# Consuming gathered expert rows two by two instead of four by four

## The chip, the cores and the metric

The program runs on one core of one Trainium2 chip. The metric is the device time of one execution in microseconds; the median of three runs of the kernel before is 1976.25 us (1974.51 to 1980.7). Engines are called as in the profile: PE is TensorE, DVE is VectorE, ACT is ScalarE, POOL is GpSimd, SP is SyncE.

## What is computed

A decoder trunk of two layers over 256 positions of width 1024, all in float32. Layer 0 mixes tokens with a state-space mixer (S5) and a GLU, layer 1 with dilated window attention (3 groups of 16 heads). After each comes PEER, a mixer that picks 128 single-neuron experts per token out of 16384 and evaluates only those:

```python
def peer_ffn(h, w_q, sub_keys, u_tab, v_tab):
    ...
    idx = jnp.take_along_axis(cand_idx, pos, axis=-1)      # 8 heads x top 16 = 128 per token
    gate = jax.nn.softmax(best, axis=-1).astype(h.dtype)
    ...
    def chunk_fn(args):
        hc, ic, gc = args
        act = jnp.einsum('cd,ckd->ck', hc, u_tab[ic])
        return jnp.einsum('ck,ckd->cd', gc * jax.nn.gelu(act), v_tab[ic])
```

So each token needs the dot product of its h with 128 rows of u, a gelu, a gate, and the sum of 128 rows of v with those weights. Rows of u and v of one expert are stored beside each other, 2048 floats.

## The kernel before

The 256 tokens are two chunks of 128. PEER is done four times (layer 0 chunks 0 and 1, layer 1 chunks 0 and 1); these are phases 0 to 3. The experts' rows of one phase are gathered while the other engines do the next chunk's mixer: phase 0 beside the S5 mixer of chunk 1, phases 1 and 2 beside projections and attention of chunks 0 and 1, phase 3 beside little else.

**A gather** (POOL, L816) brings 128 expert rows, one per partition, 8 KB each, into one of 8 slots of `ring` (`RING`, 1 MB each). The partitions are 32 tokens by 4 experts: gather j of four (`QUAD`) serves tokens 32j to 32j+31, and the four gathers with the same n serve all 128 tokens with four experts each. A phase has 128 gathers, or rows, as this text calls them for short.

**A quad** is four gathers in a row. For each, DVE waits until it has landed and takes the dot products with `Hrep`, h copied to that layout (L839, 1024 elements). After the fourth, DVE multiplies the one-hot matrix `own` with the gates from `lay` into `S` (L849), ACT takes the gelu of the 128x4 dots (L644), DVE multiplies it into `S` (L852), and PE does 8 matmuls (L380): for each half of the 1024 columns and each j, a 128x32 stationary from `S` with 512 columns of the ring slot, accumulated in partitions 32j to 32j+31 of the PSUM tile `ps`. Semaphore `v_pe` counts quads done by PE. POOL waits for it before it gathers into the slots again, four slots at a time; DVE waits for it before it writes a buffer of `S` (there are two).

**The order** is written by hand and is the same on PE, ACT and DVE. Each engine's program has a `Gather` object, and `g.at(phase, n)` stands between the pieces of the mixer: it does all gather work up to tick n, two rows a tick, 64 ticks a phase. With quads, PE and ACT have something to do only at every second tick. Each engine runs its instructions in this order. In the projections (`project`, L412; QKV has 9 of 512 columns for each half of the heads) a tick stands before each; weights come in blocks of 2 MB through two buffers of `wt`, and SP issues a load when the projection before the last is done. In the attention heads a tick stands at every second head in chunk 0 and at every head in chunk 1; a head is scores (L535), mask and maximum on DVE (L1132), exp on ACT (L729), transposes on PE (L546), their copy on ACT (L737) and the product with V (L560). PE does in a row the transposes of one head, the V products of the one before and the scores of the next but one; then it waits for DVE and ACT. In the S5 stage DVE rotates (L950 to 956), scans (L965) and forms products (L982 to 985) for 8 tiles, four ticks to a tile.

**Top-k** of the next phase's experts runs on DVE in four quarters with four parts each (`top_k_part`); a tick stands before each part. After a quarter ACT copies the result to `lay` (16 copies, L690, and a cast, L693). ACT loads a table when it changes between functions (gelu, exp, sqrt). At the start of a phase PE and ACT spread h to `Hrep` (L397, L656).

Of the kernel before, what the change touches and what calls it, by code (L numbers as in the profile page):

```python
# [29 lines left out]
ALU = mybir.AluOpType  # L30
# [3 lines left out]
P = 128  # L34
D = 1024
SEQ = 256
NC = SEQ // P
# [50 lines left out]
def build(nc, x, gains, lam, b_in, c_out, d_skip, w_glu, w_qkv, w_o, w_q, keys, experts, consts,  # L88
          masks, out):
    ctx = ExitStack()  # L90
    with ctx:
        def sb(name, shape, dt=F32):
            return ctx.enter_context(nc.sbuf_tensor(name, shape, dt))

        def sem(name):
            return ctx.enter_context(nc.semaphore(name))
# [15 lines left out]
        dots = sb("dots", [P, 2, QUAD])  # L112
        gelus = sb("gelus", [P, 2, QUAD])
        S = sb("S", [P, 2, QUAD, TG])
        zs = sb("zs", [P, 5, PAIRS])
        stat = sb("stat", [P, 8])
        half_pi = sb("half_pi", [P, 1])
# [5 lines left out]
        ps = ctx.enter_context(nc.psum_tensor("ps", [P, 8, 512], F32))  # L123
# [5 lines left out]
        own = con[:, C_REP:C_REP + TG]  # L129

        def banks(a, b):
            return ps[:, a:b, :].rearrange("p b n -> p (b n)")

        def view(t, at, *shape):
            n = int(np.prod(shape))
            v = t[:, at:at + n]
            if len(shape) == 2:
                v = v.rearrange("p (a b) -> p a b", a=shape[0])
            if len(shape) == 3:
                v = v.rearrange("p (a b c) -> p a b c", a=shape[0], b=shape[1])  # L140
            return v

        def spread(ap, axis, shape):
            return ap.unsqueeze(axis).to_broadcast(shape)
# [48 lines left out]
        ring = view(ringmem, 0, RING, 2 * D)  # L193
# [41 lines left out]
        idx_ready = sem("idx_ready")  # L235
# [2 lines left out]
        landed = [sem(f"landed{i}") for i in range(RING)]  # L238
        dots_ready = sem("dots_ready")
        gelu_ready = sem("gelu_ready")  # L240
        s_ready = sem("s_ready")
        v_pe = sem("v_pe")
        peer_done = sem("peer_done")
# [124 lines left out]
        def _(pe):  # L368
            def slot(s):

                q, j = divmod(s, QUAD)
                if j < QUAD - 1:
                    return
                phase, n = divmod(q, QUADS)
                pe.wait_ge(s_ready, q + 1)
                if n == 0 and phase:
                    pe.wait_ge(peer_done, phase)
                for half in range(2):
                    for j in range(QUAD):
                        last = pe.matmul(ps[TG * j:TG * (j + 1), half, :], S[:, q % 2, j, :],  # L380
                                         ring[:, (QUAD * q + j) % RING,
                                              D + half * 512:D + (half + 1) * 512],
                                         start=(n == 0), stop=(n == QUADS - 1), skip_group_check=True)
                last.then_inc(v_pe, 1)

# [244 lines left out]
        def _(act):  # L630
# [6 lines left out]

            def slot(s):

                q, j = divmod(s, QUAD)  # L640
                if j < QUAD - 1:
                    return
                act.wait_ge(dots_ready, q + 1)
                act.activation(gelus[:, q % 2, :], dots[:, q % 2, :],  # L644
                               ACT.Gelu_apprx_tanh).then_inc(gelu_ready, 1)

            g = Gather(slot)

            def spread_h(phase):

                if phase:
                    act.wait_ge(dots_ready, QUADS * phase)
# [150 lines left out]
        @block.gpsimd  # L803
        def _(pool):
            pool.memset(WB.rearrange("p a b c -> p (a b c)"), 0.0).then_inc(zeroed, 1)
            pool.memset(CW.rearrange("p a b c -> p (a b c)"), 0.0).then_inc(zeroed, 1)
            pool.memset(half_pi[:, :], HALF_PI).then_inc(zeroed, 1)

            for s in range(2 * NC * STEPS):
                phase, at = divmod(s, STEPS)  # L810
                n, j = divmod(at, QUAD)
                if at % QSTEPS == 0:
                    pool.wait_ge(idx_ready, QUARTERS * phase + at // QSTEPS + 1)
                if s >= RING:
                    pool.wait_ge(v_pe, (s - RING) // QUAD + 1)
                pool.indirect_dma_start(  # L816
                    ring[:, s % RING, :], None, experts[phase // NC],
                    bass.IndirectOffsetOnAxis(ap=rows[:, phase % NC, j, n:n + 1], axis=0)
                ).then_inc(landed[s % RING], 16)
# [3 lines left out]
        def _(v):  # L823
            steps = [0]

            def link(ins):
                steps[0] += 1
                ins.then_inc(dve, 1)
                v.wait_ge(dve, steps[0])

            def slot(s):

                q, j = divmod(s, QUAD)
                phase, n = divmod(q, QUADS)
                c, b, i = phase % NC, q % 2, s % RING
                if n == 0:
                    v.wait_ge(hrep_ready, 2 * QUAD * phase + 2 * j + 2)
                v.wait_ge(landed[i], 16 * (s // RING + 1))
                last = v.tensor_tensor_reduce(ring[:, i, 0:D], ring[:, i, 0:D], Hrep[:, j, :],  # L839
                                              1.0, 0.0, ALU.mult, ALU.add, dots[:, b, j:j + 1])  # L840
                if j < QUAD - 1:
# [12 lines left out]

            g = Gather(slot)
# [1 line left out]
            def peer_end(phase):  # L857

                c = phase % NC
                g.at(phase, PAIRS_G)  # L860
                v.wait_ge(v_pe, QUADS * (phase + 1))
# [406 lines left out]
```

## Time and profile before

| | |
|---|---|
| median of 3 runs | 1976.25 us |
| profiled execution, its time | 1980.83 us |
| its span | 1979.0 us |
| PE busy (matmuls) | 1131.4 us, 57% |
| DVE busy | 1220.7 us, 62% |
| ACT busy | 319.6 us, 16% |
| POOL busy | 542.8 us, 27% |
| DMA moved | 685.21 MB, mean 346 GB/s |
| mean granted clock of PE | 0.729 |

Busy times are for the whole span and mix stages with different limits. A better reading is by stretches: what PE, DVE and DMA do in 50 us of one stage. Granted clock is the share of 2.4 GHz; its two levels are 0.50 (1.2 GHz) and 1.00 (2.4 GHz). A matmul of float32 operands appears as two records, so 8 matmuls are 16 records. In a timeline the brackets hold the idle time before the row and what ended it.

### The profile page before, as it was taken

The numbers are of one execution on the slowest core, as the hardware profiler recorded it, in microseconds if no ns is written. First come the engines' busy times: TensorE is split into PE (matmuls) and PEld (weight loads), VectorE is DVE, ScalarE is ACT, GpSimd is POOL, SyncE is SP. The second block draws the span as 40 slices with busy tenths as digits, with TensorE's granted clock in tenths as the row PEclk, the third lists the DMA queues.
The fourth block names the chain that finished last, engine by engine and source line by source line (L and its number), as shares of the span: only waits on it lengthen the run. The fifth ranks groups of instructions, "written<-read, shape, count | busy, mean of one in ns | idle before, by whom it ended". The sixth has DMA issues, their size and how long they took to land.

```text
span 1979.0 us, 16308 instructions
## 1 busy us (share of the span) xinstructions
PE 1131.4 (57%) x5696; PEld 545.9 (28%) x5696; DVE 1220.7 (62%) x2986; ACT 319.6 (16%) x748; POOL 542.8 (27%) x519
## 2 busy tenths in 40 slices
PE   1568223335564786886673459688777673233232
PEld 1336001112251233434261113353354440000000
DVE  7944998885456963444455596544443567777554
ACT  4012220000111312103101122130141020011000
POOL 0001233343222222212223222322222323343332
PEclk9878556667785897896886579879867876555555
DMA  7017888889997997898899889979978988999997
GB/s 284 1 64 285 329 332 335 354 356 390 409 420 292 369 425 323 355 425 316 364 413 407 345 320 420 411 278 420 403 307 358 414 329 345 402 391 385 392 394 287
DMA packets 88642, 685.21 MB, mean 346 GB/s; under 512 B 12144, under 2 KB 12272, under 8 KB 14320
## 3 DMA queue, kind: packets, MB, share of 16 engines
q0 software_dynamic: 73728, 536.90, 68.0%
q1 hardware_dynamic: 14832, 147.26, 17.9%
q8 instruction: 45, 0.74, 0.1%
q14 instruction: 37, 0.30, 0.0%
HBM read 683.08 MB, written 1.05 MB: 346 GB/s over the span
## 4 chain that ended last, share of the span: by engine, by line
DMA 34%; PE 32%; DVE 20%; POOL 6%; issue 5%; ACT 2%; SPq 0%; POOLq 0%; DVEq 0%; ACTq 0%
DMA ringmem<-experts,lay 25%; PE ps L380 10%; PE ps L412 10%; DMA wt<-w_qkv 7%; POOL ringmem L816 6%; DVE ringmem L839 6%; PE ps L422 4%; PE ps L535 2%; DVE area L965 2%; PE ps L397 2%; PE ps L560 2%; PE ps L546 1%; DVE S L852 1%; DMA wt<-w_o 1%; DVE area L1132 1%
## 5 line engine op out<-in xcount | busy, mean ns | idle before, releaser
L816 POOL DMA_INDIRECT ringmem<-experts,lay x512 | 539.0, 1053 | 1412.2 <-PE ps L380 1115.0
L839 DVE CUSTOM_DVE_ANT_0 ringmem<-ringmem,Hrep 128x1024 f32<-128x1024 f32 x512 | 617.0, 1224 | 367.8 <-DMA ringmem<-experts,lay 357.3
L380 PE MATMUL ps<-ringmem,S 128*32 128x512 f32 x2048 | 390.9, 904 | 653.1 <-DVE S L852 653.1
L380 PEld LDWEIGHTS ps<-ringmem,S 128*32 128x32 f32 x2048 | 69.0, 143 | 906.7 <-DVE S L852 754.8
L412 PE MATMUL ps<-wt,hT 128*128 128x512 f32 x576 | 272.6, 631 | 39.2 <-DMA wt<-w_qkv 36.0
L644 ACT ACTIVATE gelus<-dots 128x4 f32<-128x4 f32 x128 | 26.3, 206 | 959.4 <-DVE dots L839 959.2
L412 PEld LDWEIGHTS ps<-wt,hT 128*128 128x128 f32 x576 | 113.9, 202 | 193.4 <-issue 189.3
L422 PE MATMUL ps<-hT,wt 128*128 128x128 f32 x1024 | 124.7, 286 | 8.1 <-DMA wt<-w_q 7.0
L422 PEld LDWEIGHTS ps<-hT,wt 128*128 128x128 f32 x1024 | 122.5, 202 | 16.9 <-DMA wt<-w_q 9.0
L1117 DVE TENSOR_TENSOR area<-ps,con 128x512 f32<-128x512 f32 x24 | 16.6, 691 | 109.4 <-PE ps L412 92.8
L1132 DVE CUSTOM_DVE_ANT_0 area<-ps,area 128x384 f32<-128x384 f32 (+1 forms) x32 | 24.2, 756 | 89.8 <-PE ps L535 89.8
L852 DVE TENSOR_TENSOR S<-S,gelus 128x128 f32<-128x128 f32 x128 | 37.5, 293 | 48.1 <-ACT gelus L644 34.3
L412 PE MATMUL ps<-wt,gT 128*128 128x512 f32 x128 | 61.3, 638 | 7.6 <-DMA wt<-w_o 3.4
L690 ACT COPY lay<-sel 32x16 f32<-32x16 f32 x256 | 51.5, 201 | 66.8 <-DVE sel L1096 64.0
L535 PE MATMUL ps<-area 64*128 64x128 f32 x288 | 55.0, 358 | 1.8 <-DVE mx L1132 1.8
L546 PE MATMUL ps<-con,area 128*128 128x128 f32 x144 | 31.2, 362 | 38.1 <-ACT area L737 37.1
L535 PEld LDWEIGHTS ps<-area 64*128 64x128 f32 x288 | 47.6, 255 | 11.9 <-issue 7.6
L560 PEld LDWEIGHTS ps<-area 128*128 128x128 f32 x288 | 48.5, 256 | 2.6 <-issue 2.5
L560 PE MATMUL ps<-area 128*128 128x64 f32 x288 | 48.9, 333 | 0.0
L644 ACT ACT_TABLE_LOAD x38 | 48.8, 1283 | 0.7
L965 DVE TENSOR_TENSOR_SCAN area<-zs,area 128x128 f32<-128x128 f32 x128 | 47.6, 435 | 0.6
L397 PE MATMUL ps<-H,con 32*128 32x512 f32 x64 | 45.6, 1017 | 3.3 <-ACT Hrep L656 3.3
(154 smaller groups left out, 1069.1 us busy)
## 6 DMA issues: line engine op xcount, KB each, us to landing
wt<-w_qkv SPq DMA_DIRECT2D x36, 2048.0 KB, 11.7
wt<-w_q SPq DMA_DIRECT2D x16, 2048.0 KB, 11.8
wt<-w_glu SPq DMA_DIRECT2D x5, 2048.0 KB, 8.2
ringmem<-experts,lay POOLq DMA_INDIRECT x512, 10.5
wt<-w_o SPq DMA_DIRECT2D x4, 2048.0 KB, 14.4
ringmem<-w_glu SPq DMA_DIRECT2D x3, 2048.0 KB, 17.0
gain<-gains SPq DMA_DIRECT2D x9, 512.0 KB, 8.8
area<-keys SPq DMA_DIRECT2D x4, 1024.0 KB, 9.5
```

The source lines that it names most:

```text
L380: last = pe.matmul(ps[TG * j:TG * (j + 1), half, :], S[:, q % 2, j, :], ring[:, (QUAD * q + j) % RING, D + half * 512:D + (half + 1) * 512 ...
L397: pe.matmul(ps[:, 2 + half, :], rep[rows_j, :], H[rows_j, half * 512:(half + 1) * 512], start=True, stop=True, skip_group_check=True).then ...
L412: last = pe.matmul(ps[:, bank, :], act[:, k, :], wt[:, n % 2, k, :], start=(k == 0), stop=(k == KT - 1))
L422: last = pe.matmul(ps[:, bank, m * P:(m + 1) * P], wt[:, n % 2, k, m * P:(m + 1) * P], hT[:, k, :], start=(k == 0 and m == 0), stop=(k == ...
L535: last = pe.matmul(ps[:, 2 + at // 512, at % 512:at % 512 + P], QT[rows, gr, h // 2, :], kt, start=True, stop=True, skip_group_check=True)
L560: last = pe.matmul(ps[:, 7, h * DH:(h + 1) * DH], PT[u % 2][:, j * P:(j + 1) * P], vv, start=(j == 0), stop=(j == n - 1), skip_group_check ...
L644: act.activation(gelus[:, q % 2, :], dots[:, q % 2, :], ACT.Gelu_apprx_tanh).then_inc(gelu_ready, 1)
L690: last = act.copy(lay[TG * r:TG * (r + 1), ph % NC, :, j, n:n + QPQ], sel[TG * j:TG * (j + 1), :, QPQ * r:QPQ * (r + 1)])
L816: pool.indirect_dma_start(ring[:, s % RING, :], None, experts[phase // NC], bass.IndirectOffsetOnAxis(ap=rows[:, phase % NC, j, n:n + 1], ...
L839: last = v.tensor_tensor_reduce(ring[:, i, 0:D], ring[:, i, 0:D], Hrep[:, j, :], 1.0, 0.0, ALU.mult, ALU.add, dots[:, b, j:j + 1])
L852: v.tensor_tensor(S[:, b], S[:, b], spread(gelus[:, b, :], 2, shape), ALU.mult).then_inc(s_ready, 1)
L965: last = v.tensor_tensor_scan(dst[:, q, :], mag[:, n:n + 1].to_broadcast([P, P]), src[:, q, :], z0[:, n:n + 1] if c else 0.0, ALU.mult, AL ...
```

## The change

The unit becomes a pair, two rows. DVE's gather work starts with the gate multiply (now 128x64) when the first row of a pair is due, before its dot, behind a wait on `v_pe` for the pair before last; a new semaphore `gated` counts it. After the second dot ACT takes a gelu of 128x2, DVE multiplies it in, and PE does 4 matmuls (two j, two halves). `v_pe` counts pairs, POOL waits per pair. `S`, `dots` and `gelus` have two buffers of half the size. All three engines now have gather work at every tick.

```diff
@@ PE
-                q, j = divmod(s, QUAD)
-                if j < QUAD - 1:
+                u, second = divmod(s, 2)
+                if not second:
                     return
...
-                pe.wait_ge(s_ready, q + 1)
+                phase, at = divmod(s, STEPS)
+                n, j = divmod(at, QUAD)
+                pe.wait_ge(s_ready, u + 1)
...
                 for half in range(2):
-                    for j in range(QUAD):
-                        last = pe.matmul(ps[TG * j:TG * (j + 1), half, :], S[:, q % 2, j, :],
-                                         ring[:, (QUAD * q + j) % RING,
-                                              D + half * 512:D + (half + 1) * 512],
+                    for i in range(2):
+                        t = j - 1 + i
+                        last = pe.matmul(ps[TG * t:TG * (t + 1), half, :], S[:, u % 2, i, :],
+                                         ring[:, (2 * u + i) % RING, D + half * 512:D + (half + 1) * 512],
@@ ACT
-                act.wait_ge(dots_ready, q + 1)
-                act.activation(gelus[:, q % 2, :], dots[:, q % 2, :],
+                act.wait_ge(dots_ready, u + 1)
+                act.activation(gelus[:, u % 2, :], dots[:, u % 2, :],
                                ACT.Gelu_apprx_tanh).then_inc(gelu_ready, 1)
@@ POOL
-                    pool.wait_ge(v_pe, (s - RING) // QUAD + 1)
+                    pool.wait_ge(v_pe, (s - RING) // 2 + 1)
@@ DVE
+                if not second:
+                    if at % QSTEPS == 0:
+                        v.wait_ge(idx_ready, QUARTERS * phase + at // QSTEPS + 1)
+                    if u >= 2:
+                        v.wait_ge(v_pe, u - 1)
+                    shape = [P, 2, TG]
+                    v.tensor_tensor(S[:, b], spread(own, 1, shape),
+                                    spread(lay[:, c, 1, j:j + 2, n], 2, shape), ALU.mult).then_inc(gated, 1)
...
                 v.wait_ge(landed[i], 16 * (s // RING + 1))
                 last = v.tensor_tensor_reduce(ring[:, i, 0:D], ring[:, i, 0:D], Hrep[:, j, :],
-                                              1.0, 0.0, ALU.mult, ALU.add, dots[:, b, j:j + 1])
-                if j < QUAD - 1:
+                                              1.0, 0.0, ALU.mult, ALU.add, dots[:, b, second:second + 1])
+                if not second:
                     return
                 last.then_inc(dots_ready, 1)
-                if n % QPQ == 0:
-                    v.wait_ge(idx_ready, QUARTERS * phase + n // QPQ + 1)
-                if q >= 2:
-                    v.wait_ge(v_pe, q - 1)
-                shape = [P, QUAD, TG]
-                link(v.tensor_tensor(S[:, b], spread(own, 1, shape), spread(lay[:, c, 1, :, n], 2, shape),
-                                     ALU.mult))
-                v.wait_ge(gelu_ready, q + 1)
-                v.tensor_tensor(S[:, b], S[:, b], spread(gelus[:, b, :], 2, shape),
+                v.wait_ge(gated, u + 1)
+                v.wait_ge(gelu_ready, u + 1)
+                v.tensor_tensor(S[:, b], S[:, b], spread(gelus[:, b, :], 2, [P, 2, TG]),
                                 ALU.mult).then_inc(s_ready, 1)
```

The places that wait for whole phases (`spread_h` on ACT, `peer_end` on DVE) count pairs instead of quads. In the changed kernel line 380 is line 383, 412 is 414, 535 is 537, 546 is 548, 560 is 562, 839 is 850, 849 is 845 and 852 is 857.

On PE, in the attention heads of chunk 1 (second layer), before: transposes, V products, scores, and a quad at every second head.

```order
L546 MATMUL ps<-con,area 128x128 x6
L560 MATMUL ps<-area 128x64 x6
L535 MATMUL ps<-area 128x128 x6
L380 MATMUL ps<-ringmem,S 32x512 x8
L546 MATMUL ps<-con,area 128x128 x6
L560 MATMUL ps<-area 128x64 x6
L535 MATMUL ps<-area 128x128 x6
L546 MATMUL ps<-con,area 128x128 x6
L560 MATMUL ps<-area 128x64 x6
L535 MATMUL ps<-area 128x128 x6
L380 MATMUL ps<-ringmem,S 32x512 x8
```

The same place after.

```order
L548 MATMUL ps<-con,area 128x128 x6
L562 MATMUL ps<-area 128x64 x6
L537 MATMUL ps<-area 128x128 x6
L383 MATMUL ps<-ringmem,S 32x512 x4
L548 MATMUL ps<-con,area 128x128 x6
L562 MATMUL ps<-area 128x64 x6
L537 MATMUL ps<-area 128x128 x6
L383 MATMUL ps<-ringmem,S 32x512 x4
```

Four matmuls stand between any two heads now, where eight stood between every second two.

On DVE, at the end of a quarter of top-k in phase 0 (`sel` is the quarter's result), before: the two dots are followed by the next quarter's maxima.

```order
L1096 TENSOR_TENSOR sel<-qs 128x32
L839 ISA ringmem,dots<-ringmem,Hrep 128x1024
L839 ISA dots 128x1
L839 ISA ringmem,dots<-ringmem,Hrep 128x1024
L839 ISA dots 128x1
L1032 MAX qs<-ps 128x8 x4
```

The same place after (`L1101` and `L1037` are the old 1096 and 1032).

```order
L1101 TENSOR_TENSOR sel<-qs 128x32
L845 TENSOR_TENSOR S<-con,lay 128x64
L850 ISA ringmem,dots<-ringmem,Hrep 128x1024
L850 ISA dots 128x1
L850 ISA ringmem,dots<-ringmem,Hrep 128x1024
L850 ISA dots 128x1
L857 TENSOR_TENSOR S<-S,gelus 128x64
L1037 MAX qs<-ps 128x8 x4
```

Both multiplies into `S` now stand around these two dots, and the second waits for ACT's gelu with the maxima behind it.

## Rows read from the trace of the kernel before

**Rows 1.** From the page: the last chain, L380's group, the gathers' queue.

```profile
DMA 34%; PE 32%; DVE 20%; POOL 6%; issue 5%; ACT 2%; SPq 0%; POOLq 0%; DVEq 0%; ACTq 0%
...
L380 PE MATMUL ps<-ringmem,S 128*32 128x512 f32 x2048 | 390.9, 904 | 653.1 <-DVE S L852 653.1
...
q0 software_dynamic: 73728, 536.90, 68.0%
```

**Rows 2.** Stretches: length; busy us of PE, PEld, DVE, ACT, POOL; PEclk; DMA share; GB/s.

```profile
200.00:250.00 50.00, 14.23 (x64) 2.38 (x64) 48.14 (x156) 9.90 (x33) 14.18 (x15) 0.53 0.84 317
...
850.00:900.00 50.00, 41.71 (x135) 17.15 (x133) 20.00 (x38) 3.73 (x8) 12.06 (x12) 0.91 1.01 421
...
1450.00:1500.00 50.00, 43.18 (x258) 32.51 (x256) 21.60 (x47) 18.49 (x27) 13.13 (x14) 0.72 0.68 253
1626.00:1967.00 341.00, 116.43 (x505) 20.05 (x504) 217.86 (x515) 30.76 (x99) 124.85 (x120) 0.57 0.96 383
```

**Rows 3.** VectorE's waits, 300:450, then 1626:1800: total us, times, longest.

```profile
DVE ringmem L839 <- DMA ringmem<-experts,lay: 17.0, 19, 1.8
...
DVE ringmem L839 <- DMA ringmem<-experts,lay: 40.7, 35, 2.6
```

**Rows 4.** Timeline of PE: start, us, line, shapes, records; a quad cold, one warm, a projection.

```profile
1719.88 3.64 PE L380 MATMUL ps<-ringmem,S 128*32 128x512 f32 x16 [7.23 <-DVE S L852]
...
834.65 1.92 PE L380 MATMUL ps<-ringmem,S 128*32 128x512 f32 x16
836.50 7.13 PE L412 MATMUL ps<-wt,hT 128*128 128x512 f32 x16
```

**Rows 5.** Table of stretches again: Hrep's copies, a cold head, a warm head.

```profile
610.00:621.00 11.00, 11.00 (x16) 3.70 (x14) 4.66 (x8) 4.10 (x7) 5.01 (x4) 0.50 0.98 396
...
1449.00:1455.50 6.50, 6.50 (x30) 6.16 (x29) 0.64 (x4) 2.40 (x3) 0.00 (x0) 0.50 0.99 389
1457.70:1462.30 4.60, 4.39 (x38) 3.44 (x30) 1.35 (x4) 0.82 (x3) 2.92 (x3) 1.00 0.40 123
```

**Rows 6.** Timeline of PE in the heads of chunk 1.

```profile
1465.41 1.51 PE L546 MATMUL ps<-con,area 128*128 128x128 f32 x6 [3.08 <-ACT area L737]
...
1472.17 3.15 PE L380 MATMUL ps<-ringmem,S 128*32 128x512 f32 x16
1475.32 0.85 PE L546 MATMUL ps<-con,area 128*128 128x128 f32 x6
...
1482.07 1.51 PE L546 MATMUL ps<-con,area 128*128 128x128 f32 x6 [3.08 <-ACT area L737]
```

**Rows 7.** Timeline of PE in the heads of chunk 0.

```profile
781.04 0.87 PE L546 MATMUL ps<-con,area 128*128 128x128 f32 x3 [2.05 <-ACT area L737]
...
784.59 3.64 PE L380 MATMUL ps<-ringmem,S 128*32 128x512 f32 x16
788.16 0.74 PE L546 MATMUL ps<-con,area 128*128 128x128 f32 x3
```

**Rows 8.** Timeline of VectorE and ScalarE after a quarter of top-k.

```profile
222.13 3.40 ACT L690 COPY lay<-sel 32x16 f32<-32x16 f32 x16 [4.60 <-DVE sel L1096]
...
225.79 1.28 ACT L644 ACT_TABLE_LOAD   x1
...
229.78 0.28 DVE L849 TENSOR_TENSOR S<-con,lay 128x128 f32<-128x128 f32 x1
...
230.21 0.29 DVE L852 TENSOR_TENSOR S<-S,gelus 128x128 f32<-128x128 f32 x1
...
230.41 0.87 DVE L1041 MAX8 qs<-gT 128x8 f32<-128x128 f32 x4
```

**Rows 9.** Last chain, in order of time: quads in the S5 stage.

```profile
321.57 3.36 PE ps L380 x16
...
413.94 3.68 PE ps L380 x16
```

**Rows 10.** Timeline of PE: a projection that waited for weights.

```profile
856.74 8.80 PE L412 MATMUL ps<-wt,hT 128*128 128x512 f32 x16 [1.98 <-DMA wt<-w_qkv]
```

More of the change, by code:

```diff
@@ L111, in build @@
         rows = lay[:, :, 0].bitcast(U32)
-        dots = sb("dots", [P, 2, QUAD])
-        gelus = sb("gelus", [P, 2, QUAD])
-        S = sb("S", [P, 2, QUAD, TG])
+        dots = sb("dots", [P, 2, 2])
+        gelus = sb("gelus", [P, 2, 2])
+        S = sb("S", [P, 2, 2, TG])
         zs = sb("zs", [P, 5, PAIRS])
@@ L240, in build @@
         gelu_ready = sem("gelu_ready")
+        gated = sem("gated")
         s_ready = sem("s_ready")
@@ L369, in slot @@
             def slot(s):
-                q, j = divmod(s, QUAD)
-                if j < QUAD - 1:
+                u, second = divmod(s, 2)
+                if not second:
                     return
-                phase, n = divmod(q, QUADS)
-                pe.wait_ge(s_ready, q + 1)
+                phase, at = divmod(s, STEPS)
+                n, j = divmod(at, QUAD)
+                pe.wait_ge(s_ready, u + 1)
                 if n == 0 and phase:
@@ L638, in slot @@
             def slot(s):
-                q, j = divmod(s, QUAD)
-                if j < QUAD - 1:
+                u, second = divmod(s, 2)
+                if not second:
                     return
-                act.wait_ge(dots_ready, q + 1)
-                act.activation(gelus[:, q % 2, :], dots[:, q % 2, :],
+                act.wait_ge(dots_ready, u + 1)
+                act.activation(gelus[:, u % 2, :], dots[:, u % 2, :],
                                ACT.Gelu_apprx_tanh).then_inc(gelu_ready, 1)
@@ L651, in spread_h @@
                 if phase:
-                    act.wait_ge(dots_ready, QUADS * phase)
+                    act.wait_ge(dots_ready, PAIRS_G * phase)
                 for j in range(QUAD):
@@ L831, in slot @@
             def slot(s):
-                q, j = divmod(s, QUAD)
-                phase, n = divmod(q, QUADS)
-                c, b, i = phase % NC, q % 2, s % RING
+                u, second = divmod(s, 2)
+                phase, at = divmod(s, STEPS)
+                n, j = divmod(at, QUAD)
+                c, b, i = phase % NC, u % 2, s % RING
+                if not second:
[6 more added lines that the diff above has]
+                                    spread(lay[:, c, 1, j:j + 2, n], 2, shape), ALU.mult).then_inc(gated, 1)
                 if n == 0:
@@ L839, in slot @@
                 last = v.tensor_tensor_reduce(ring[:, i, 0:D], ring[:, i, 0:D], Hrep[:, j, :],
-                                              1.0, 0.0, ALU.mult, ALU.add, dots[:, b, j:j + 1])
-                if j < QUAD - 1:
+                                              1.0, 0.0, ALU.mult, ALU.add, dots[:, b, second:second + 1])
+                if not second:
                     return
                 last.then_inc(dots_ready, 1)
-                if n % QPQ == 0:
-                    v.wait_ge(idx_ready, QUARTERS * phase + n // QPQ + 1)
-                if q >= 2:
-                    v.wait_ge(v_pe, q - 1)
-                shape = [P, QUAD, TG]
-                link(v.tensor_tensor(S[:, b], spread(own, 1, shape), spread(lay[:, c, 1, :, n], 2, shape),
-                                     ALU.mult))
-                v.wait_ge(gelu_ready, q + 1)
-                v.tensor_tensor(S[:, b], S[:, b], spread(gelus[:, b, :], 2, shape),
+                v.wait_ge(gated, u + 1)
+                v.wait_ge(gelu_ready, u + 1)
+                v.tensor_tensor(S[:, b], S[:, b], spread(gelus[:, b, :], 2, [P, 2, TG]),
                                 ALU.mult).then_inc(s_ready, 1)
@@ L860, in peer_end @@
                 g.at(phase, PAIRS_G)
-                v.wait_ge(v_pe, QUADS * (phase + 1))
+                v.wait_ge(v_pe, PAIRS_G * (phase + 1))
                 v.tensor_tensor(X[:, c, :], X[:, c, :], banks(0, 2), ALU.add).then_inc(peer_done, 1)
```

## Prediction

> **What bounds the kernel now.** I read the page first, then the table of stretches, then the timeline of the places where the limit changes. The page says that TensorE's scaling-matrix matmuls (L380, 128 quads) are busy for 390.9 us, and that the last chain is shared by DMA 34%, PE 32% and DVE 20% [rows 1]. So no single engine sets the end: the stages have different limits, and the edit has to be priced in each of them. The table of stretches [rows 2] shows four kinds. Around 200 to 250 VectorE is busy 48.1 of 50 us while DMA moves 317 GB/s: VectorE bounds. At 850 to 900 (projections) DMA is at share 1.01 and 421 GB/s: DMA bounds, with PE close behind at 41.7 of 50. At 1450 to 1500 (attention heads of chunk 1) DMA is at 0.68 and no engine is full: the chain score, mask, exp, transpose, times V bounds, through PE. From 1626 to 1967 (last PEER phase) DMA is at 0.96 and 383 GB/s: nearly DMA, with small gaps from the ring. An edit to the gather path can gain only where the ring limits DMA; elsewhere it can only cost.
>
> **What stays.** Bytes, gathers (512), dots (512), POOL's issues and the order of everything that isn't gather work stay. What moves is the grain: gelu, S and matmuls come 256 times for two rows, not 128 times for four, and slots are released two at a time.
>
> **The ring: the gain.** Now four slots come free at once, after the fourth row's dot, gelu, S and 3.64 us of L380; with only four rows queued behind, DMA runs dry briefly. 512 gathers moved 536.9 MB [rows 1], so a gather is 1.05 MB; 128 of them at 421 GB/s need 319 us, and the last phase took 341 [rows 2]: at most 22 us. Released by twos, the queue still holds six rows (about 15 us) while two are worked on for some 6 us, so DMA should not run dry. Against that, the extra VectorE work below eats part of its slack of 40.7 us in DMA waits [rows 3]. I take 18 us gained, bounds 8 and 22. The other stages that DMA bounds are at 1.01 already and give nothing.
>
> **PE: each pair costs what a quad cost.** A quad's 8 matmuls (16 records) take 3.64 us at the 1.2 GHz level and 1.92 us at the 2.4 GHz level; 16 records of a full-width projection of the same 512 columns take 7.13 at 2.4 GHz [rows 4]. So the four 32-column matmuls of a half run at the same time, one per column strip. A pair has two strips of the four to fill: each strip still streams its two halves one after the other. So I take 3.64 and 1.92 us per pair, no less than per quad: L380 goes from 391 to nearly 800 us. The trace has no row with two strips, so the lower bound is half of each (1.82 and 0.96). The Trainium skill ("TensorEngine Tiling (Array Packing)", Performance Considerations) says that 32-column stationaries give up to four tiles at once; by it the pair uses half of that, which agrees with my choice.
>
> **Clock.** In the heads of chunk 1 PE stayed at 0.50 through 6.5 us of unbroken transposes, V products and scores, and was at 1.00 in the head that followed a quad's L380; at the start of the second PEER phase it stayed at 0.50 through 11 us of unbroken L397, which fills 32 of 128 rows [rows 5]. The one thing that lifted it among heads was four strips of L380 at once. A pair fills two. I take it that pairs don't lift it, and that the heads run at 1.2 GHz throughout.
>
> **Attention, chunk 1: +33.** A head without the higher clock takes 1472.17 - 1465.41 = 6.76 us of PE work, then a gap of 3.08 us in which VectorE and ScalarE do mask, exp and a copy; the quad's L380 lies in that gap and just fits (1472.17 to 1475.32). The next head runs fast and with its gap takes 6.75 [rows 6]. Mean of the two: (9.91 + 6.75)/2 = 8.33. After, every head has an L380 of 3.64, longer than the gap: 6.76 + 3.64 = 10.4. 16 heads at 2.07 is 33 us.
>
> **Attention, chunk 0: +12, and +5.** Its heads take 3.56 us of PE and a gap of 2.05; a quad's L380 of 3.57 fills the gap and stands 1.5 out of it, and the next head starts fast [rows 7]: by the ratio in chunk 1 (3.67 against 6.76) 1.9, with its gap 4.0. Four heads now: 5.6 + 5.6 + 7.1 + 4.0 = 22.3. After, with a pair every second head: 5.6 + 7.1, twice, is 25.4. 0.78 per head, 16 heads: 12. At the ends of the four half blocks a few pairs meet no gap at all, 3.64 each; part falls into waits for rows. I take 5 (0 to 14).
>
> **VectorE-bound stretches: +27.** Per quad VectorE now spends 229.78 to 230.41 = 0.63 us from the last dot to the next work [rows 8]. After, each pair has a first multiply (half as wide, some 0.13 us more) and then dot end to S, 0.43, and S, 0.13: 0.69 per pair, 1.38 per quad. That's 0.38 more per pair. Second, a new wait: after each quarter of top-k ScalarE does 16 copies (3.40 from 222.13), the cast and a gelu table load (225.79 to 227.07). Now the dots of the next two rows are followed by other top-k work, and the gelu's wait comes only after the quad's last dot at 229.78. After, the dots end near 224.4 and VectorE waits in order for the gelu near 227.3: 2.5 us, and the top-k work queued behind it waits too. First phase: 12 ticks at 0.38 and three quarters at 2.5 is 12; in the two middle phases a rope covers one wait and the last ticks are DMA's, so 7.5 each. In the last phase both fall into VectorE's DMA waits.
>
> **S5 beside the first phase: +9.** Four periods of 8 rows lie between the quads at 321.57 and 413.94, 23.1 us each [rows 9], with some 2.6 of DMA wait (17.0 in 150 us) [rows 3]. So 20.5 of work, 1.5 added: 22.0. But PE is cold: S waits for the L380 two pairs back, and the rotation of the next step waits for its matmuls behind a 3.64 us L380: 1.0 + 1.1. 24.2 against 23.1, eight periods: +9 (-9 if PE is quick, +16 if each pair stalls).
>
> **Projections: +8.** Per two ticks two projections, turns and one L380 stand against 19.8 us of DMA; PE waits 1.98 for weights and then starts cold (8.80 instead of 7.13) [rows 4, 10]. A second L380 of 1.92 mostly fits into that wait. 18 pairs of ticks at 0.45: 8 (0 to 35, if all of it shows). What is queued behind the new PE wait for S is the projection itself, and behind its end SP's next weight load.
>
> **Sum.** -18 + 33 + 12 + 5 + 27 + 9 + 8 = +76 us. The profiled run took 1980.83 (span 1979.0), so 2056.8; against the median of 1976.25, 2052.
>
> **Rivals.**
> Pairs are cheap on PE (1.82 and 0.96 us, strips or halves overlapping after all): the attention terms are then 0, the S5 term -9, projections 0: -18 + 27 - 9 = 0, so 1976, no change. For it: nothing but the missing row. Against: 3.64 for 16 records is already four at once. 0.07.
> The clock stays high: every gap now holds an L380, so PE idles 1.2 us per head, not 3.08. Each head of chunk 1 then takes 6.75, -25; chunk 0 some 4.7, -15; S5 -9, ring -22, VectorE +27, projections 0: -44, so 1932. It decides where PE stays at 1.00 from head to head. Against it: 11 us of unbroken work at 0.50 [rows 5]. The Trainium skill ("TensorE: Matmul & The Clock Gate", HAM oscillation) blames idle gaps for the low clock, by which this rival would be right; the rows speak against it. 0.11.
> PE becomes the bound in the projections, and S5 stalls at each pair: the terms 8 and 9 become 35 and 16: 2086. For it: PE is at 41.7 of 50 already. 0.12.
> The forecast, 0.70, with what lies next to it: the range 1990 to 2088 leaves out the first two rivals, 0.18. Its low end is the sum with the ring at 22, the loose pairs at 0, S5 at -9 and half of chunk 1's and chunk 0's loss: 76 - 4 - 5 - 18 - 22 - 13 (half of VectorE's 27) = 14, which is 1990; its high end is the third rival.
>
> **Chances.** A measurement of this kernel tells about 0.3% (6 us) from no change. Faster by more: 0.11. Within: 0.07. Slower: 0.82.
>
> **What the profile will show.** L380 with 2048 records and 700 us busy or more, median L380 burst of 8 records 3.64 or 1.92. Granted clock near 0.50 in all heads, heads of chunk 1 about 10.4 us apart. VectorE waits for gelu: three of 2.5 us before 300 us. The last phase 320 to 330 us with DMA near 410 GB/s. Wrong would be: bursts near 1.9 us at clock 0.50 (first rival), or 1.00 through the heads (second).

## The result and the profile after

The changed kernel takes 1917.59 us (median of 4 runs, 1913.54 to 1919.38) against 1978.47 us for four executions of the kernel before measured with it (1974.51 to 1982.74). The ratio is 0.9689, 95% interval [0.9661, 0.9717]: it is 3.1% faster, where I forecast 3.8% slower and a range from 1990 up. The profiled execution took 1913.54 us with a span of 1911.8.

I read the page of after first. Its columns are those of [rows 1].

```profile
L818 POOL DMA_INDIRECT ringmem<-experts,lay x512 | 593.4, 1159 | 1288.5 <-PE ps L383 1014.2
L383 PE MATMUL ps<-ringmem,S 128*32 128x512 f32 x2048 | 642.1, 772 | 441.9 <-DVE S L857 441.8
...
L857 DVE TENSOR_TENSOR S<-S,gelus 128x64 f32<-128x64 f32 x256 | 57.6, 225 | 182.9 <-ACT gelus L646 182.9
```

L383 has as many records as L380 had, but is busy 642.1 us instead of 390.9, and its mean fell from 904 to 772 ns. The first number says that pairs are dear, the second that more of them run at the higher clock. VectorE waits 182.9 us in all for the gelu of the pairs, where it waited 34.3 for that of the quads. So two of the costs that I forecast are there. What I didn't forecast shows in VectorE's waits over the whole span (total us, times, longest). Before:

```profile
DVE ringmem L839 <- DMA ringmem<-experts,lay: 357.3, 233, 6.1
```

After, the gelu stands first and the rows second.

```profile
DVE S L857 <- ACT gelus L646: 182.9, 256, 5.8
DVE ringmem L850 <- DMA ringmem<-experts,lay: 136.6, 132, 4.0
```

VectorE waited 357.3 us for gathered rows and now waits 136.6: 220 us less. Phase by phase the wait was 73.5, 93.7, 75.0 and 115.0 us and is 22.7, 33.2, 19.5 and 61.1. And the timeline of PE in the heads of chunk 1, the place of [rows 6]:

```profile
1425.79 1.91 PE L383 MATMUL ps<-ringmem,S 128*32 128x512 f32 x8
1428.94 0.85 PE L548 MATMUL ps<-con,area 128*128 128x128 f32 x6 [1.24 <-ACT area L739]
...
1432.53 1.91 PE L383 MATMUL ps<-ringmem,S 128*32 128x512 f32 x8
1435.69 0.85 PE L548 MATMUL ps<-con,area 128*128 128x128 f32 x6 [1.24 <-ACT area L739]
...
1442.43 0.85 PE L548 MATMUL ps<-con,area 128*128 128x128 f32 x6 [1.24 <-ACT area L739]
```

Every head starts with transposes of 0.85 us where every second one took 1.51. The heads are 6.75 us apart (1435.69 - 1428.94), where I forecast 10.4. The table of stretches gives the same for the second block of eight of these heads (columns of [rows 2]), and in the second row the first block of chunk 0's heads:

```profile
1398.00:1464.00 66.00, 54.03 (x346) 33.09 (x344) 42.08 (x99) 37.68 (x53) 27.82 (x26) 0.97 0.97 390
...
755.00:816.00 61.00, 47.76 (x209) 24.17 (x206) 30.11 (x79) 23.14 (x42) 19.63 (x19) 0.86 0.90 356
```

Before, over the same stretch:

```profile
755.00:816.00 61.00, 43.04 (x190) 25.88 (x191) 26.57 (x64) 15.91 (x33) 14.57 (x16) 0.66 0.72 284
```

The granted clock is 0.97 in these heads of chunk 1, and 0.86 against 0.66 in those of chunk 0; DMA moves 356 GB/s there instead of 284. In chunk 0's heads the clock still changes: transposes of three matmuls stand there at 0.52 us and at 0.87.

**A ruler for the experiments.** Hrep's copies (L397, in after L399) start each phase, so their first rows cut the span into four phases that can be compared between kernels. (Phase 0 of every later kernel is counted from 177.0; its first copy starts between 174.7 and 177.3, which leaves up to 2 us open in that phase.) Before:

```profile
177.30:609.50 432.20, 189.94 (x1282) 83.22 (x1281) 316.27 (x747) 55.47 (x162) 137.95 (x132) 0.68 0.91 365
609.50:1116.70 507.20, 346.79 (x1453) 171.36 (x1449) 274.00 (x692) 89.45 (x211) 133.22 (x128) 0.76 0.91 369
1116.70:1620.20 503.50, 372.55 (x1692) 200.46 (x1688) 279.24 (x692) 106.86 (x217) 139.25 (x128) 0.80 0.90 362
1620.20:1979.00 358.80, 125.87 (x532) 23.08 (x528) 225.00 (x527) 34.21 (x105) 128.60 (x124) 0.57 0.93 372
```

After:

```profile
177.00:613.90 436.90, 264.76 (x1284) 92.92 (x1282) 322.32 (x811) 62.20 (x194) 151.55 (x134) 0.73 0.91 361
613.90:1098.90 485.00, 384.64 (x1451) 166.24 (x1449) 279.75 (x756) 105.50 (x251) 149.80 (x128) 0.88 0.94 387
1098.90:1569.40 470.50, 394.34 (x1691) 188.23 (x1689) 284.88 (x756) 131.15 (x263) 144.11 (x128) 0.92 0.96 388
1569.40:1911.80 342.40, 183.67 (x530) 33.72 (x528) 231.31 (x591) 40.55 (x137) 147.91 (x123) 0.76 0.94 387
```

This execution of before is some 14 us longer in the four phases together than those in which an experiment left a phase with quads: there phase 0 took 427.8 to 429.2 us, phase 1 501.8 to 503.6, phase 2 501.0 and 501.2, phase 3 355.5 to 355.7. I compare with the middle of those: 428.5, 502.7, 501.1, 355.6. Against them after has +8.4, -17.7, -30.6 and -13.2 us. These are single executions: two kernels whose phase 1 was pairs from end to end took 485.0 and 491.1 us there, so a phase is known to some 6 us only, and each verdict below is taken from the ratio of timed runs.

### The profile page after: what moved, and what is told of

It is laid out like the page before. It is cut to its first block, busy times and chain, and to the rows that moved or that the text cites. A ratio compares the mean times of both kernels' runs of the same rounds, so it can differ in the third digit from the quotient of the medians.

```text
span 1911.8 us, 16847 instructions
## 1 busy us (share of the span) xinstructions
PE 1322.5 (69%) x5696; PEld 548.2 (29%) x5696; DVE 1244.5 (65%) x3242; ACT 372.8 (20%) x898; POOL 597.1 (31%) x519
## 4 chain that ended last, share of the span: by engine, by line
PE 37%; DMA 26%; DVE 26%; ACT 5%; issue 4%; POOL 1%; DVEq 0%; SPq 0%; POOLq 0%
DMA ringmem<-experts,lay 17%; PE ps L383 12%; PE ps L414 11%; DVE ringmem L850 7%; PE ps L424 5%; DMA wt<-w_qkv 5%; DVE area L970 2%; PE ps L399 2%; DMA wt<-w_q 2%; PE ps L537 2%; ACT lay L692 2%; DMA wt<-w_o 2%; PE ps L562 2%; POOL ringmem L818 1%; PE ps L548 1%
## 5 line engine op out<-in xcount | busy, mean ns | idle before, releaser
L818 POOL DMA_INDIRECT ringmem<-experts,lay x512 | 593.4, 1159 | 1288.5 <-PE ps L383 1014.2
L383 PE MATMUL ps<-ringmem,S 128*32 128x512 f32 x2048 | 642.1, 772 | 441.9 <-DVE S L857 441.8
L850 DVE CUSTOM_DVE_ANT_0 ringmem<-ringmem,Hrep 128x1024 f32<-128x1024 f32 x512 | 612.7, 1222 | 139.5 <-DMA ringmem<-experts,lay 136.6
L383 PEld LDWEIGHTS ps<-ringmem,S 128*32 128x32 f32 x2048 | 115.2, 128 | 887.4 <-DVE S L857 629.3
L414 PE MATMUL ps<-wt,hT 128*128 128x512 f32 x576 | 257.7, 601 | 11.2 <-DMA wt<-w_qkv 11.1
L646 ACT ACTIVATE gelus<-dots 128x2 f32<-128x2 f32 x256 | 52.2, 204 | 985.2 <-DVE dots L850 984.5
L857 DVE TENSOR_TENSOR S<-S,gelus 128x64 f32<-128x64 f32 x256 | 57.6, 225 | 182.9 <-ACT gelus L646 182.9
L845 DVE TENSOR_TENSOR S<-con,lay 128x64 f32<-128x64 f32 x256 | 56.7, 221 | 31.1 <-PE ps L383 29.6
L414 PE MATMUL ps<-wt,gT 128*128 128x512 f32 x128 | 62.5, 645 | 11.3 <-DMA wt<-w_o 10.4
L470 PE MATMUL ps<-area 128*32 128x128 f32 x512 | 22.6, 326 | 36.9 <-DVE area L990 36.9
L1037 DVE MAX8 qs<-ps 128x8 f32<-128x128 f32 x64 | 14.2, 284 | 47.5 <-PE ps L445 47.5
L399 PE MATMUL ps<-H,con 32*128 32x512 f32 x64 | 41.3, 882 | 3.3 <-ACT Hrep L658 3.3
L537 PE MATMUL ps<-area 64*128 64x128 f32 x288 | 43.5, 303 | 0.0
```

The costliest lines, as they stand in the source:

```text
L383: last = pe.matmul(ps[TG * t:TG * (t + 1), half, :], S[:, u % 2, i, :], ring[:, (2 * u + i) % RING, D + half * 512:D + (half + 1) * 512], ...
L399: pe.matmul(ps[:, 2 + half, :], rep[rows_j, :], H[rows_j, half * 512:(half + 1) * 512], start=True, stop=True, skip_group_check=True).then ...
L414: last = pe.matmul(ps[:, bank, :], act[:, k, :], wt[:, n % 2, k, :], start=(k == 0), stop=(k == KT - 1))
L537: last = pe.matmul(ps[:, 2 + at // 512, at % 512:at % 512 + P], QT[rows, gr, h // 2, :], kt, start=True, stop=True, skip_group_check=True)
L646: act.activation(gelus[:, u % 2, :], dots[:, u % 2, :], ACT.Gelu_apprx_tanh).then_inc(gelu_ready, 1)
L818: pool.indirect_dma_start(ring[:, s % RING, :], None, experts[phase // NC], bass.IndirectOffsetOnAxis(ap=rows[:, phase % NC, j, n:n + 1], ...
```

## The experiments

All were made from one kernel, in which a function says for each phase and tick whether the two rows belong to a quad or to a pair. With 4 everywhere it does what the kernel before does, with 2 everywhere what the changed one does. Its L399 is L380 of before and L383 of after, its L872 the dots (L839 and L850); with the ring of 6 slots they are L400 and L873.

### Does a pair's shape lift the clock?

The kernel before with quads, and in chunk 1's heads four matmuls of constants at each tick where no quad is due, in the shape of a pair (two strips, 128 rows, 512 columns, two halves). They write a free part of PSUM; nothing is left out.

```diff
+            def idle(rows):
+                for _ in range(2):
+                    for t in range(2):
+                        pe.matmul(ps[TG * t:TG * (t + 1), 4, :], con[0:rows, C_REP:C_REP + TG],
+                                  con[0:rows, 0:512], start=True, stop=True, skip_group_check=True)
...
+                        if c == 1 and 1 <= i < NH + 2 and (base + i) % 2:
+                            idle(P)
```

> The kernel before, quads everywhere, with one thing added: in chunk 1's attention heads PE also does, at the ticks without a quad, four matmuls of a pair's shape (128 rows, two strips of 32 columns, 512 columns) on constants, into a PSUM bank that nothing reads. Output unchanged. Theory A (a pair's matmuls in every gap keep TensorE at 2.4 GHz, and that is where the change gained in attention): granted clock 1.00 from head to head, heads 6.75 us apart instead of 9.91 and 6.75, 8 heads less by 3.1 us, minus a few loose groups of 1.9 at the ends: 15 to 25 us faster, 1953 to 1963. Theory B (the gain in the heads comes from rows that land earlier, not from the clock): no head gets shorter, 0 to 10 us slower.

1949.12 us against 1970.58, ratio 0.9899 [0.9876, 0.9922]: 20 us gained by work that computes nothing. The timeline of PE:

```profile
1439.23 1.91 PE L547 MATMUL ps<-con 128*32 128x512 f32 x8
1442.38 0.85 PE L570 MATMUL ps<-con,area 128*128 128x128 f32 x6 [1.24 <-ACT area L764]
...
1445.97 1.92 PE L399 MATMUL ps<-ringmem,S 128*32 128x512 f32 x16
1449.13 0.85 PE L570 MATMUL ps<-con,area 128*128 128x128 f32 x6 [1.23 <-ACT area L764]
```

The heads look as in after, 6.75 us apart. Phase 2 took 480.6 us instead of 501.1, and the other phases are unchanged. The gain is in the range that I expected (15 to 25 us); the absolute times were counted from a slower execution of before. The pair's two strips hold the clock as the quad's four do. That pairs also raise it shows in phase 3 of after, where PE does little but L383: the mean clock is 0.76 there, against 0.57 before.

The same with only 32 of the 128 rows, `idle(32)`:

> As the run with the added groups, but each added matmul has a stationary and moving operand of 32 partitions instead of 128, the same columns and the same duration. Output unchanged. If what I read from Hrep's L397 matmuls (11 us at 0.50 with 32 rows) carries over, these don't lift the clock: heads stay at 9.9 and 6.75 us or get 0.6 longer, 0 to 8 us slower than before. If any unbroken work in the gap does it, as idle gaps being the cause would have it, the time equals the other run's within 5 us.

1971.29 us against 1970.58, ratio 1.001 [0.9985, 1.0036]: nothing.

```profile
1453.48 1.91 PE L547 MATMUL ps<-con 32*32 32x512 f32 x8
1456.63 1.51 PE L570 MATMUL ps<-con,area 128*128 128x128 f32 x6 [1.24 <-ACT area L764]
...
1463.39 3.27 PE L399 MATMUL ps<-ringmem,S 128*32 128x512 f32 x16
1466.59 0.88 PE L570 MATMUL ps<-con,area 128*128 128x128 f32 x6
```

The gap is closed to the same 1.24 us, and PE is as long busy; still the next head runs at 1.51 us for its transposes, the lower level, until a quad comes. So what fell was my evidence: L397 at 0.50 for 11 us [rows 5] was about matmuls that fill 32 rows, and I had read it as being about PE work in general. My other row, 6.5 us of transposes, V products and scores at 0.50, stands: in the 32-row run the same head again runs unbroken at the lower level from 1456.63 until the quad. Those matmuls have 64 or 128 rows, so the number of rows alone doesn't account for it, and no run here tells what does. The Trainium skill ("TensorE: Matmul & The Clock Gate", HAM oscillation) explains a clock that falls by the idle gaps between bursts of matmuls. The 128-row run agrees with it (gap 3.08 to 1.24 us, clock up); the 32-row run doesn't, since its gaps are the same 1.24 us and its clock still fell. What the two runs show is that the gap alone doesn't decide it.

### What is the early release of slots worth?

Pairs everywhere, but POOL waits for the second pair of four rows, so slots come free by fours:

```diff
-                    pool.wait_ge(v_pe, UNIT_OF[s - RING] + 1)
+                    pool.wait_ge(v_pe, UNIT_OF[(s - RING) | 3] + 1)
```

> The changed kernel (pairs on DVE, ACT and PE), but POOL gathers into the slots of a quad again only when both its pairs are done: the ring is released by fours as before. Output unchanged. Theory A (clock and PE in attention, projections): keeps the gain of phases 1 and 2 and loses the 14 us of phase 3 and some 10 elsewhere: 1935 to 1950. Theory B (early release of slots is the whole gain): no gain, and the costs on VectorE stay: 1985 to 2005.

1983.79 us against 1970.58, ratio 1.0081 [1.0055, 1.0108]. The theory that the clock is nearly the whole gain (1935 to 1950) falls; the one that the release is the larger part (1985 to 2005) is 1.2 us off the edge of its range. One line of the change turns 3.1% faster into 0.8% slower. Its phases (same columns):

```profile
177.00:630.10 453.10, 267.23 (x1279) 93.16 (x1277) 322.15 (x809) 61.62 (x192) 144.87 (x132) 0.72 0.86 347
630.10:1135.30 505.20, 391.04 (x1451) 169.41 (x1449) 280.81 (x756) 105.60 (x251) 134.59 (x128) 0.86 0.90 370
1135.30:1619.30 484.00, 395.01 (x1691) 187.96 (x1689) 286.13 (x756) 131.12 (x263) 139.19 (x128) 0.92 0.92 376
1619.30:1975.60 356.30, 189.87 (x530) 33.66 (x528) 231.80 (x591) 40.55 (x137) 137.56 (x125) 0.71 0.94 378
```

Against after, each phase is longer: by 16.2, 20.2, 13.5 and 13.9 us, 64 in all (66 between the two medians, 77 by the two ratios). VectorE's waits for rows are at 271.2 us instead of 136.6:

```profile
DVE ringmem L872 <- DMA ringmem<-experts,lay: 271.2, 196, 6.2
```

The mean clock is nearly that of after, 0.819 to 0.836. The release is thus the larger part of the gain, and it is worth about the same in each phase, also in those where I had put it at nothing.

If free slots are what counts, fewer slots must hurt. Pairs, released by twos, with a ring of 6 slots instead of 8:

```diff
-RING = 8
+RING = 6
+RINGMEM = 8
...
-        ringmem = sb("ringmem", [P, RING * 2 * D])
+        ringmem = sb("ringmem", [P, RINGMEM * 2 * D])
```

> The changed kernel with pairs everywhere, but with 6 slots in the ring instead of 8; nothing else differs. Output unchanged. If release by twos gains because fewer slots sit taken while their quad isn't done (quads hold 4 to 8 of the 8 in use for transfers, pairs of 6 hold 4 to 6, about as many on average), it gives the same as the run that released by fours with 8 slots, 1984 +- 12. If the gain is that gathers are issued more evenly, whatever the depth, most of it stays: below 1945.

2009.54 us against 1972.18, ratio 1.0199 [1.018, 1.0219]: 92 us above after, and 26 above the kernel with 8 slots released by fours. The waits for rows (same view as above):

```profile
DVE ringmem L873 <- DMA ringmem<-experts,lay: 311.8, 221, 7.6
```

This is neither of the two results that I expected: it is 14 us above the upper edge of 1984 +- 12, and far from the 1945 of an effect of evenness. So the number of slots counts, and for more than my count of taken slots gave. Against after its phases are longer by 18, 27, 10 and 31 us. The depth of the queue is a limit over the whole kernel.

### Is it the order of the strips?

Quads, but with the 16 records ordered as two pairs of strips (j 0 and 1 for both halves, then 2 and 3), which is the order in which a pair has them:

```diff
-                for half in range(2):
-                    for j in range(QUAD):
+                for two in range(0, size, 2):
+                    for half, i in ((0, two), (0, two + 1), (1, two), (1, two + 1)):
```

> The kernel before, quads everywhere, but the eight matmuls of a quad are ordered as two pairs (both halves of strips 0 and 1, then both of strips 2 and 3), so that only two strips can run at once. Same work, same releases. Output unchanged. If two strips cost what four cost, 16 records take 7.1 us at 1.2 GHz and 3.8 at 2.4 instead of 3.64 and 1.92; if not, they stay. In time: releases come 1.9 to 3.5 us later, phase 3 is up to 30 us longer, against a higher clock in the heads: 1975 to 2010.

1973.51 us against 1970.58, ratio 1.0017 [1.0001, 1.0034], and a quad's 16 records keep their length (592, 1061 and 1064 ns as the shortest, median and longest record), as does the whole quad when cold:

```profile
1701.36 3.64 PE L399 MATMUL ps<-ringmem,S 128*32 128x512 f32 x16 [6.42 <-DVE S L887]
```

The order makes no difference that matters, so this run says nothing on what two strips alone cost. After itself does, in phase 3, where PE's clock changes often:

```profile
1850.49 1.91 PE L383 MATMUL ps<-ringmem,S 128*32 128x512 f32 x8 [1.34 <-DVE S L857]
...
1860.44 3.43 PE L383 MATMUL ps<-ringmem,S 128*32 128x512 f32 x8 [2.53 <-DVE S L857]
```

Eight records take what sixteen took [rows 4], 1.91 warm. In the cold 3.43 the clock rose before the end; unbroken cold ones are at 3.63:

```profile
219.72 3.63 PE L383 MATMUL ps<-ringmem,S 128*32 128x512 f32 x8 [3.68 <-DVE S L857]
```

### Where do pairs gain, where do they lose?

Pairs in phase 3 alone, quads elsewhere:

```diff
-    return 2
+    return 2 if phase == 3 else 4
```

> Pairs in phase 3 alone, quads in phases 0 to 2. Output unchanged. The stages add up if this gives phase 3's share of the whole and no more: 14 us less than before (327 against 341), 1957 to 1963. If phase 3's gain came from the stages ahead (the state in which the ring is handed over), less than 8.

1957.58 us against 1972.18, ratio 0.9936 [0.9917, 0.9956], 12.6 us less (8.7 to 16.4). Phase 3 took 341.9 us, as in after, instead of 355.6.

Pairs only around the attention heads of both chunks:

```diff
-    return 2
+    return 2 if phase == 1 and (16 <= tick < 24 or 34 <= tick < 40) or \
+        phase == 2 and (16 <= tick < 28 or 38 <= tick < 50) else 4
```

> Pairs only around the attention heads: ticks 16 to 24 and 34 to 40 of phase 1, 16 to 28 and 38 to 50 of phase 2; quads elsewhere. Output unchanged. The clock (20 us by the run with the added groups) and the earlier releases in these stretches together (6.6 and 13.4 us in chunk 1's, 3.5 and 5.9 in chunk 0's stretches between before and after): 25 to 32 us faster, 1940 to 1948. If the clock is all there is to gain in the heads: 1950.

1940.45 us against 1972.18, ratio 0.9849 [0.983, 0.9868], 29.8 us less. Phase 1 went from 502.7 to 498.9 and phase 2 from 501.1 to 476.0. Of the 30 us, 20 are the clock in chunk 1's heads by the run with constants. The other 10 lie in the same ticks; whether they come from earlier rows or from the clock in chunk 0's heads no run separates.

Pairs in phase 0 alone:

```diff
-    return 2
+    return 2 if phase == 0 else 4
```

> Pairs in phase 0 alone (the first 128 gathers), quads in the other three phases. This tests whether VectorE's extra work and the earlier release are two effects that add up in one phase. Theory: between the last rows of ticks 0, 16, 40 and 64 the changed kernel stood at 116.0, 138.0 and 167.3 us against 102.1, 139.5 and 176.9 before, so VectorE loses 14 and the ring gives back 11; the sum is about +3 us, 1975 to 1985 and phase 0's first ticks at 116. Rival: the loss in the first ticks is not VectorE's own but comes from something that all phases share; then the first ticks stay near 102 and the time is 1960 to 1970.

1979.51 us against 1967.92, ratio 1.0058 [1.0037, 1.0079]: pairs lose 7 to 16 us in phase 0. The sum that I expected from single executions, +3, was too small; its sign and place were right. How many dots VectorE has done in the first 136 us of the phase shows it (length; DVE busy us with records; clock; DMA share; GB/s), for the dots' line alone. Before:

```profile
177.00:313.00 136.00, 45.33 (x76) 0.58 0.84 321
```

With pairs in phase 0:

```profile
177.00:313.00 136.00, 40.31 (x68) 0.56 0.81 307
```

Five us fewer of dots at 1.22 us each are four dots that haven't been reached. Before, a dot came every 3.6 us here (38 in 136 us), so that is some 14 us behind. VectorE isn't busier, it waits for the gelu. Its waits in the first ticks before:

```profile
DVE S L852 <- ACT gelus L644: 0.5, 1, 0.5
```

After:

```profile
DVE S L857 <- ACT gelus L646: 14.9, 16, 2.9
```

With pairs in phase 0 alone the same wait is 15.3 us, and in the kernel of the next section, which keeps quads here, 1.5. The rest of the phase gives only a part of it back.

### A kernel that keeps quads where VectorE is full

Quads while top-k's quarters fill VectorE (ticks 0 to 16 of phase 0, 0 to 12 of phases 1 and 2), pairs in the rest:

```diff
-    return 2
+    return 4 if tick < (16, 12, 12, 0)[phase] else 2
```

> The changed kernel, but with quads at the ticks that share VectorE with top-k: ticks 0 to 16 of phase 0, 0 to 12 of phases 1 and 2. Pairs everywhere else. Output unchanged. If the first ticks lose to the pairs' two extra costs on VectorE (the narrower multiplies and the wait for the gelu behind ScalarE's copies; 14 us in phase 0, 3.4 and 4.0 in the first 8 ticks of phases 1 and 2) and release by twos gives nothing there, they come back: 1896 to 1903. If release by twos gains as much there as VectorE loses, 1915 to 1920.

1904.78 us against 1972.18, ratio 0.9647 [0.963, 0.9664]. That is 1.8 us above the range of the first theory (1896 to 1903) and 10 below that of the second. After is at 0.9689 [0.9661, 0.9717]: by the ratios the mixed kernel is some 8 us faster than after, but the two intervals just touch. Its phase 0 and phase 1:

```profile
177.00:599.90 422.90, 237.79 (x1279) 88.38 (x1277) 320.10 (x794) 60.03 (x184) 154.83 (x134) 0.73 0.92 373
599.90:1091.80 491.90, 382.88 (x1451) 169.55 (x1449) 278.41 (x744) 104.42 (x245) 146.75 (x128) 0.84 0.93 381
```

Phase 0 gains 14 us on after's 436.9. Phase 1 gains nothing by keeping quads: 491.9 against 485.0. I took that for a hint that VectorE's loss there is given back later, and kept the quads only in ticks 0 to 16 of phase 0 and 0 to 8 of phase 2:

```diff
-    return 4 if tick < (16, 12, 12, 0)[phase] else 2
+    return 4 if tick < (16, 0, 8, 0)[phase] else 2
```

> Quads only where top-k fills VectorE and nothing is given back later: ticks 0 to 16 of phase 0 and 0 to 8 of phase 2; pairs everywhere else. Theory (VectorE's extra work in the first ticks of phases 1 and 2 is partly lent, since the same kernel with quads up to tick 12 of phase 1 was slower at ticks 8 to 32 than the kernel with pairs throughout): the time is 3 to 6 us under the first mixed kernel's 1904.8, so about 1900. Rival (a loss in VectorE's stretches is a loss for good): 3 to 5 us over it, about 1909.

1904.45 us against 1967.92, ratio 0.9671 [0.9645, 0.9697]. Neither number came: the median is the first mixed kernel's and the two intervals overlap; this one overlaps after's too. Its phase 1, pairs throughout as in after, took 491.1 us and not 485.0, so the hint was scatter. Phase 0 is 14 us shorter than in after in both mixed kernels (422.9 and 422.2). Phase 2 took 470.7 us with quads up to tick 12, 472.3 up to tick 8 and 470.5 with none. In phases 1 and 2 it makes no measurable difference which grain the first ticks have.

## Why the prediction was wrong

Set side by side (us, each phase against phases with quads):

| phase | pairs, slots by fours | slots by twos, the rest of it | after in all |
|---|---|---|---|
| 0 | +24.6 | -16.2 | +8.4 |
| 1 | +2.5 | -20.2 | -17.7 |
| 2 | -17.1 | -13.5 | -30.6 |
| 3 | +0.7 | -13.9 | -13.2 |
| sum | +10.7 | -63.8 | -53.1 |

The timed runs make the last sum 61 us (56 to 67 by the ratio's interval). The two columns aren't two independent effects: with slots by fours the clock in chunk 0's first heads is 0.77, with slots by twos 0.86, so a part of what the clock gives hangs on the release.

**The ring: the term was mis-sized, -18 against some -64.** For phase 3 it held: -13 to -14 for the phase, with DMA at 400 GB/s where I forecast 410, and 327 us for the stretch that took 341 before [rows 2]:

```profile
1573.00:1900.00 327.00, 176.65 (x513) 31.92 (x512) 224.39 (x581) 37.10 (x131) 145.12 (x120) 0.75 0.97 400
```

What failed is the sentence "The other stages that DMA bounds are at 1.01 already and give nothing", with the one before it, that an edit to the gather path gains "only where the ring limits DMA; elsewhere it can only cost". At 850 to 900 it is true; after shows the same share and rate there:

```profile
850.00:900.00 50.00, 45.30 (x151) 17.58 (x149) 24.52 (x55) 7.13 (x16) 17.90 (x14) 1.00 1.01 421
```

But I took 50 us of one stage for a whole kind of stage. Over the whole of phases 0 to 2 the share before was 0.90 to 0.91 and the rate 362 to 369 GB/s, and VectorE waited for rows 357.3 us in all. That one row, read ahead and split by phase (73.5, 93.7, 75.0, 115.0), would have shown that rows come late in each phase. With slots released by twos phases 1 and 2 went to 387 and 388 GB/s, against 370 and 376 by fours. That a slot waiting for the other half of its quad can't take a gather when DMA has a moment free is my reading of it; that the number of free slots counts, the ring of 6 showed.

**PE: right.** "Each pair costs what a quad cost" holds: 1.91 and 3.63 us. L383 is at 642.1 us instead of the nearly 800 of the text, and below the 700 that I named as a sign; that is the clock.

**Clock: this step failed.** "I take it that pairs don't lift it, and that the heads run at 1.2 GHz throughout." They run at 1.00, and the constants showed that two strips do it without any other part of the change. **Attention chunk 1, +33,** was this step's consequence and measured -20 in the run with constants; the rival had worked out -25 for it. **Chunk 0, +12 and +5:** phase 1 as a whole has +2.5 us without the release and 3.8 us less with pairs around its heads, so there is no loss of that size; the clock there went from 0.66 to 0.86.

**VectorE, +27: right in phase 0, not found in phases 1 and 2.** The wait that I named is there, and it is 2.87 us long where I had 2.5. Three of them stand after quarters of top-k before 300 us (2.87, 2.86, 2.87), as forecast; a fourth, of 2.26, stands at 200.05, where ACT copies `hT` and loads a table before the gelu. One of the three:

```profile
228.93 1.28 ACT L646 ACT_TABLE_LOAD   x1
230.23 0.20 ACT L646 ACTIVATE gelus<-dots 128x2 f32<-128x2 f32 x1
230.53 0.23 DVE L857 TENSOR_TENSOR S<-S,gelus 128x64 f32<-128x64 f32 x1 [2.87 <-ACT gelus L646]
```

The kernel that keeps the quads there is 14 us shorter in phase 0; the term said 12. The 7.5 each for phases 1 and 2 can't be found: phase 1 took 491.9 us with quads in its first ticks and 485.0 and 491.1 without, phase 2 took 470.7 with and 470.5 without.

**S5, +9: about right, and hidden by the release.** The S5 ticks (16 to 40 of phase 0) took 139 us before, 147 with pairs and slots by fours, and 138 in after. Over the whole of phase 0 pairs with slots by fours lost 24.6 us, and the release gives 16 back.

**Projections, +8:** without the release phase 1, heads included, lost 2.5 us, no more than it scatters. The cold start that the term rested on (8.80 us [rows 10]) has gone with the clock, which is 1.00 at 850 to 900 instead of 0.91.

The rival "the clock stays high" named the right clock, 1.00 through the heads, and gave 1932, 14 us above what came. That it came so near is in part luck: its ring, -22, was as wrong as mine, 42 us too small. Against that stood a gain of 9 in S5, where pairs cost 8, and a gain of 40 in the heads, of which the run with constants shows 20 and the run with pairs around the heads, release included, 30. The forecast wasn't saved by its costs being real: it missed by 137 us (+76 against -61): 50 for losses in the heads that didn't come, 20 for what the clock gives in chunk 1, 46 for the ring; the 21 left are about the size of VectorE's and the projections' terms that weren't found. What stays open is how the remaining gain of the clock divides among chunk 0's heads, turns and projections; none of the runs changes the clock there alone.

## What to carry to other kernels

A wait for buffers summed over the whole span and by stage (here 357 us on rows) shows where a finer release can gain, though it isn't itself the gain: the release took 135 us off the wait and some 64 off the time. One stretch at full DMA rate says nothing about the stage around it. Before you take a row as evidence that some work doesn't lift the clock, ask in what it differs from the work that you are pricing: L397 fills 32 rows and the pairs' matmuls 128, and two kernels whose added matmuls differ in this alone came out 22 us apart. And a finer grain is best bought by stages: quads where an engine that works in order would wait for the finer grain, pairs where slots are short, gave 3.5% and 3.3% in two kernels against 3.1%, with phase 0 shorter by 14 us in both; the intervals of the whole just touch or overlap.

## What the runs showed of the hardware

- Two column strips of 32 with 128 rows took as long as four: 8 records in 1.91 us, 16 in 1.92, at the higher clock. The order of the matmuls among the strips made no difference (ratio 1.0017).
- Matmuls with 128 rows and two strips held the clock between heads, and the same number of matmuls of the same length with 32 rows didn't: 1949.12 and 1971.29 us for two kernels that differ in nothing else.
- Adding 1.91 us of useless matmuls at every second head made the kernel 1% faster. A gap of 1.24 us was left in both kernels, so an idle gap isn't the whole of what decides.
